# A tile of expert rows shared by two consecutive pairs in the sum into tokens

## The reference

```python
top_val, top_idx = lax.top_k(logits, TOP_K)              # TOP_K = 2, of 8 experts
gates = jax.nn.softmax(top_val, axis=-1)
combine = jnp.sum(jax.nn.one_hot(top_idx, N_EXPERTS) * gates[..., None], axis=1)
for e in range(N_EXPERTS):                               # t is 256 x 1024, experts 3584 wide
    out = out + combine[:, e:e + 1] * (silu(t @ w_gate[e]) * (t @ w_up[e])) @ w_down[e]
```

## Time and profile before

| What | us |
|---|---|
| time, median of 3 runs | 1363.96 |
| lowest and highest of them | 1361.51, 1366.25 |
| time of the profiled execution | 1361.95 |
| its span, first to last instruction | 1360.5 |

### The profile page before, as it was taken

One profiled execution on the slowest core, in us unless ns is written; L12 is line 12 of the kernel. 1 busy time (PEld: TensorE's weight loads), 2 busy tenths in 40 slices (PEclk: granted clock), 3 DMA queues, 4 the chain that ended last, 5 costly groups with the idle time before them and its releaser, 6 DMA issues.

```text
span 1360.5 us, 20505 instructions
## 1 busy us (share of the span) xinstructions
PE 1297.9 (95%) x8957; PEld 811.9 (60%) x8957; DVE 553.3 (41%) x804; ACT 442.7 (33%) x658; POOL 10.8 (1%) x35
## 2 busy tenths in 40 slices
PE   7989999998988999899799999999999999999997
PEld 6777788877777666667666484733333354333343
DVE  5674455545585654646566474410000001200003
ACT  6554444436552553535346263300000000000001
POOL 3000000000000000000000000000000000000000
PEclk9989999999988999899899999999999999999999
DMA  9335555374102999999999999999999999999992
GB/s 333 118 124 185 186 187 186 121 247 145 41 1 89 409 409 390 408 361 395 407 385 407 383 408 402 402 409 409 408 409 396 381 363 347 391 379 404 406 398 82
DMA packets 129067, 418.75 MB, mean 308 GB/s; under 512 B 4248, under 2 KB 8384, under 8 KB 128976
## 3 DMA queue, kind: packets, MB, share of 16 engines
q1 hardware_dynamic: 127872, 416.30, 79.2%
q0 software_dynamic: 544, 1.12, 0.3%
q10 hardware_dynamic: 560, 0.01, 0.0%
HBM read 416.37 MB, written 1.05 MB: 307 GB/s over the span
## 4 chain that ended last, share of the span: by engine, by line
PE 87%; DVE 5%; DMA 3%; ACT 3%; issue 1%; ACTq 0%; SPq 0%; DVEq 0%
PE bank L2036 26%; PE bank L2107 14%; PE bank L1694 13%; PE bank L1695 13%; PE bank L1696 13%; DMA ring<-in_moe_w_down 3%; PE bank L1972 2%; PE bank L1966 2%; PE bank L2055 1%; ACT raw_d L776 1%; DVE lo L1083 1%; DVE mx L1172 1%; DVE raw_d L1169 1%; DVE w_lo L1513 1%; PE bank L1803 1%; PE bank L1744 1%
## 5 line engine op out<-in xcount | busy, mean ns | idle before, releaser
L1513 DVE TENSOR_TENSOR w_lo<-ring,w_hi 128x1024 fp32r<-128x1024 f32 x168 | 202.1, 1224 | 69.5 <-ACT w_hi L711 61.7
L2036 PE MATMUL bank<-ring,late_acts 128*32 128x256 f32 (+3 forms) x1936 | 215.8, 434 | 0.0
L711 ACT ACTIVATE w_hi<-ring 128x1024 fp32r<-128x1024 f32 x168 | 174.9, 1058 | 101.1 <-PE bank L1696 77.8
L1694 PE MATMUL bank<-hi,act_hi 128*128 128x512 f32 (+1 forms) x400 | 156.1, 390 | 12.6 <-DVE lo L1083 6.6
L2036 PEld LDWEIGHTS bank<-ring,late_acts 128*32 128x32 f32 (+1 forms) x1936 | 85.7, 120 | 121.6 <-issue 100.8
L2107 PE MATMUL bank<-ring,at_buf 128*32 128x256 f32 (+1 forms) x1408 | 157.1, 450 | 0.5 <-ACT at_buf L711 0.5
L1695 PE MATMUL bank<-lo,act_hi 128*128 128x512 f32 (+1 forms) x400 | 153.9, 385 | 0.0
L1696 PE MATMUL bank<-hi,act_lo 128*128 128x512 f32 (+1 forms) x400 | 153.8, 384 | 0.0
L711 ACT ACTIVATE at_buf<-bank 128x256 f32<-128x256 f32 (+2 forms) x40 | 18.0, 450 | 412.7 <-PE bank L2055 412.7
L1083 DVE TENSOR_TENSOR lo<-raw_gu,hi 128x1024 fp32r<-128x1024 f32 x96 | 112.4, 1221 | 25.7 <-ACT hi L711 25.0
L1535 DVE TENSOR_TENSOR silu_buf<-silu_buf,bank 128x512 f32<-128x512 f32 (+2 forms) x56 | 29.4, 536 | 225.5 <-PE bank L2036 192.2
(11 more groups left out here) (240 smaller groups left out, 1272.0 us busy)
## 6 DMA issues: line engine op xcount, KB each, us to landing
ring<-in_moe_w_up SPq DMA_DIRECT2D x50, 2048.0 KB, 15.5
ring<-in_moe_w_down SPq DMA_DIRECT2D x49, 2048.0 KB, 15.6
ring<-in_moe_w_gate SPq DMA_DIRECT2D x48, 2048.0 KB, 15.1
raw_gu<-in_w_in SPq DMA_DIRECT2D x7, 2048.0 KB, 13.1
ring_after<-in_moe_w_gate SPq DMA_DIRECT2D x7, 2048.0 KB, 15.8
ring_after<-in_moe_w_down SPq DMA_DIRECT2D x7, 2048.0 KB, 16.9
ring_after<-in_moe_w_up SPq DMA_DIRECT2D x6, 2048.0 KB, 16.8
raw_gu<-in_dense_w_gate SPq DMA_DIRECT2D x5, 2048.0 KB, 8.1
```

Of the source, the lines that this page charges most:

```text
L711: return nc.scalar.activation(out, in_, ACT.Copy, **kw)
L1513: v.tensor_tensor(w_lo[:, n % WP, :], flat(u)[:, q * 1024:(q + 1) * 1024], w_hi[:, n % WP, :], ALU.subtract).then_inc(w_lo_done, 1)
L1694: mm(out, ah, wh, start=start, stop=False, **kw)
L2036: ins = mm(bank[b][c * g.n:(c + 1) * g.n, 0:width], acts[STEPS[s][0]][:, k, g.col:g.col + g.n], by_rows(u, n)[:, kl, c * width:(c + 1) * w ...
```

## The change

Of the slots of two consecutive pairs (0 with 1, and 2 with 3), the second tile is now one and the same. The table `ROW_OF` gives each group (pair, expert, group) its tile and first row. Pair 0 puts its 32 slots of rank 7 and the last 32 of rank 0 in rows 0 to 63 of tile 1, as before. Pair 1 now puts its rank 6 in rows 64 to 127 of it, where it used rows 0 to 63. In pair 2 the 32 odd slots of rank 4 go to rows 96 to 127 of tile 0, and its other 64 stay in tile 1; pair 3 puts its rank 5 in rows 64 to 127 of tile 1.

```diff
+ROW_OF = {(0, 0, 0): (0, 0), (0, 0, 1): (0, 64), (0, 0, 2): (1, 32), (0, 1, 0): (1, 0),
+          (1, 0, 0): (0, 0), (1, 0, 1): (0, 64), (1, 1, 0): (1, 64),
+          (2, 0, 0): (0, 0), (2, 0, 1): (0, 64), (2, 1, 1): (0, 96), (2, 1, 0): (1, 0),
+          (3, 0, 0): (0, 0), (3, 0, 1): (0, 64), (3, 1, 0): (1, 64)}
...
-        self.tile, self.row = w, 64 * i
-        if w == 0 and i == 2:
-            self.tile, self.row = 1, CAPS[PAIRS[p][1]]
+        self.tile, self.row = ROW_OF[p, w, i]
...
     if n < 8:
+        if p % 2 == 1:
+            return ("rows", 0, n - 4) if n >= 4 else None
         return ("rows", n // 4, n % 4) if p > 0 else None
-    if n in (8, 9):
+    if n == 8 or (n == 9 and p % 2 == 1):
         return ("gates", n - 8, 0)
...
-                        if a == 1 and p < NP - 1:
+                        if a == p % 2 and p < NP - 1:
                             build_gsel(p + 1)
...
-                        pe.wait_ge(y_out, 2 * (p - 1) + a + 1)
+                        pe.wait_ge(y_out, 2 * p if p % 2 == 1 or a == 1 else 2 * p - 1)
```

## The result

| Kernel | median of 5 runs, us | lowest, highest |
|---|---|---|
| before | 1364.47 | 1361.51, 1366.25 |
| changed | 1353.88 | 1352.08, 1357.11 |

The ratio is 0.9926 (95% interval 0.9906 to 0.9947), which is 10.1 us less, between 7.2 and 12.8. The forecast was 1356.2, in a range of 1353.8 to 1361.1; the median lies 0.1 us inside its lower end. The profiled execution of the changed kernel took 1353.63 us, 1351.7 of it span.

What follows compares the result with a forecast made beforehand. PE was taken to bound the kernel, with the loads close behind. Terms 3.8 + 4.2 + 0.3 = 8.3 us, less 0.5 for loads, gave 7.8 us less: 1354.1 profiled, 1356.2 against the median, range 1353.8 to 1361.1.

Steps and rivals of the forecast that it cites:

- Row products of pair 1: Four row products (extras 0 to 3) leave PE's stream in pair 1, nothing taking their place: 3.83 us less.
- extra 0: First of pair 1's four removed row products, in step 8 between gate and up products: 0.86 us on the chain.
- More rows contracted: Remaining products contract over 128 rows instead of 64 or 96, in pair 2 and at the end: 0 cost.
- Row products of pair 3: Four row products leave PE's stream in pair 3, at 1.05 us each: 4.2 us less, called safe from the loads.
- Gate turn of pair 2: One turn of gates (two transposes) goes in pair 2, where PE never idles: 0.3 us less.
- That of pair 0: One turn of gates goes in pair 0, ahead of a wait for loads: 0, and 0.3 us at most.
- Turn at the end of step 8: PE's turn of gated values has less work ahead, some 0.4 us cover left: 0 cost, 0.5 us if not.
- Builds moved: In pair 0 DVE's six builds move ahead of two subtractions, with 1.4 us of cover: 0, at most 0.1 us.
- Loads: Pair 1, ahead of its last wide down products: loads nearly follow the faster PE, 0.5 us lost, between 0 and 3.8.
- Rival (a): Loads don't close up; PE waits 3.8 us in pair 1, perhaps at half clock: 1359.5 to 1361.1 us, chance 0.18.
- Rival (b): Loads bound all of the experts' part, so a faster PE only waits more: 1364.0 us, chance 0.07.
- Rival (c): Slower: PE waits at pair 1's wide down products, each wait halving the clock and costing 1.6 us more; chance 0.03.

Runs made afterwards that it cites:

- k128: Kernel before, products summing pairs 0 and 1 padded with zero rows to contract over 128, none removed: 0.81 us less at extras 4 to 7, 0.33 in pair 2.
- before2: The kernel before, unchanged, profiled a second time: 1362.51 us in one run.
- again2: The changed kernel, unchanged, in a third profile: 1353.20 us in its one run.
- again: The changed kernel, unchanged, timed and profiled once more: 1355.26 us, median of 6, against 1362.66 for the kernel before, ratio 0.9942.
- norows1: The changed kernel without the four row products of pair 1 (pair 0's tile 0 not added to the tokens): 1353.68 us in one run.
- late_norows: The changed kernel with DVE's down-sum copies behind step 8's first low pieces and pair 1's four row products left out: 1346.84 us in one run.
- late_before: The kernel before, with DVE's down-sum copies moved behind the low pieces of step 8's first unit: 1357.59 us, ratio 0.9963 to before.

## Why the prediction was right

The sum was 7.8 us off the profiled time, and 8.3 were measured between the two profiled executions (1361.95 to 1353.63), and 10.1 and 7.9 by the ratios of all runs. The mechanism is the one that was named: products leave a PE that hardly stops, and the loads keep up. But the number is better than the terms: on PE 8.8 us were won where 8.3 were forecast, in these two executions none of the 0.5 for the loads was lost, and 0.5 came back outside the span. Step by step:

- **Row products of pair 1, 3.83 forecast.** The intervals gave 0.01 for extra 0 and 2.97 for extras 1 to 3. The three were right (0.86 + 1.05 + 1.06 = 2.97). Extra 0 failed: the chain gave it 0.86 us, but the product covered ACT's silu, and a wait of 0.78 us took its place. The step that failed is the sentence that nothing takes their place, with "followed by wide products, which start without the pause" as the reading of a short entry. The short entry was the sign of the cover.
- **More rows contracted, 0 forecast.** It was a gain of 0.82 us in pair 1 and 0.33 in pair 2, and the eight products at the end took 0.19 less (no run pads those alone). The mistake was to price a product by the duration of its records where its cost lies in the distances to its neighbours.
- These two errors nearly cancel, by luck: -0.86 and +1.34.
- **Row products of pair 3, 4.2 forecast.** 4.23.
- **Gate turn of pair 2, 0.3 forecast.** 0.67 less the 0.33 that k128 shows for the rows: 0.34. **That of pair 0, 0 forecast:** 208.18 and 207.71 for 0 to 39 against 207.80; nothing that can be told.
- **Turn at the end of step 8, 0 forecast.** No wait in PE's timeline of the changed kernel:

```profile
701.06 1.93 PE L2113 MATMUL bank<-ring,at_buf 128*32 128x256 f32 x32
...
702.93 0.66 PE L2061 MATMUL bank<-ident,silu_buf 128*128 128x128 f32 x4
```

- **Builds moved, 0 forecast.** The copy and the subtraction are 3.30 us apart (539.81 to 543.11), as before (537.47 to 540.77 in the earlier trace rows), and DVE still waits 1.54 us in between:

```profile
539.81 0.43 DVE L1485 COPY gselT<-bank 128x256 f32<-128x256 f32 x1 [3.37 <-PE bank L1994]
540.15 1.42 DVE L1466 TENSOR_SCALAR gsel<-iota,slot_r,gate_r 128x64 f32<-128x64 f32 x6
543.11 0.69 DVE L1527 TENSOR_TENSOR at_wide_lo<-bank,at_wide_hi 128x512 fp32r<-128x512 f32 x1 [1.54 <-ACT at_wide_hi L717]
```

- **Loads, 0.5 lost forecast, between 0 and 3.8.** 0 in two profiles and 1.55 in one. The reading of the earlier trace rows was right: the gap between the loads that landed at 755.2 and 762.1 closed (756.3 and 761.5 in the changed kernel). The reading of the earlier trace rows, that no cover at all is left, was true of that one execution only. In before2 there were 2.7 us of it, and the loads needed to follow by less than the 3.8 us: they came 2.0 us earlier in again2, and cover paid the rest. So nothing is lost where the parts of the load lie close, and "again" shows an execution in which the last two were late.

Rival (a), that the loads don't close up, didn't come. The wait in "again", at the place that it named, cost 1.5 us and no clock; its cause was the spread of one load's parts and not a full queue. Rival (b), that the loads bound everything, is excluded by 4.23 us won in pair 3. In pair 1 it is nearly true of the changed kernel, which had 1.3 us left (norows1), and wholly true once DVE's copies are later: late_norows shows products worth 4.3 us leaving for nothing. Rival (c) didn't come: no stretch of PE's work behind 681 us was at half clock in the changed kernel.

The sum has nothing of the start and of the part behind PE. The first row of the table varies by 2.3 us without a pattern. The last is near 7.8 in all kernels with a shared tile and 8.9 to 9.3 in those without; all of that 1.1 us lies behind the last instruction of DVE, and about 0.5 comes back outside the span. Why it goes with the sharing stays open, and it wasn't tried.

## What to carry to other kernels

Before an operation is counted as gained, look at what its successor waits for: if the chain shows it shorter than its neighbours of the same kind, it is probably covering a wait, and moving work into that place is worth more than taking it out of it. Price an operation on a pipelined engine by the distance from the product ahead to the one behind, with and without it, and not by the duration of its record. Where loads run near their limit, measure the cover at the tightest point, from the landing to PE's arrival: it (1.3 us here) says how much more work is worth removing before the loads have to be relieved first. Take it from more than one profile, for the last part of one load can land 2.7 us late in one profile and not in the next.

## What the runs showed of the hardware

- Products over 64 rows between products over 128 rows cost up to 0.28 us more at their borders than the same product over 128 rows, though the records have one duration. Beside products that are themselves over 64 rows (as at 965 us in pair 2) the row product takes 1.05 to 1.06 us to its neighbour in both forms.
- One core drew 409 to 410 GB/s from its loads for tens of microseconds.
- The 16 parts in which a 2 MB load lands lay 2.0 us apart in one profile of a kernel and 4.7 in another (changed and "again", unit 82; 4.3 and 2.2 in the kernel before and before2). What waits for the load waits for the last of them.
- The same short wait can leave the clock alone or halve it. In the kernel before PE waited 1.33 us at 735 and stayed at 1.00. In late_before it waited as long at 730, and behind it the clock stood at 0.50 (1.2 GHz) for 3.4 us, which cost 1.6. PE's timeline and the stretch behind it (columns as in the earlier trace rows) in late_before:

```profile
730.21 0.50 PE L1701 MATMUL bank<-w_hi,wide_hi 128*128 128x512 f32 x1 [1.33 <-DVE w_lo L1513]
...
730.70:733.90 3.20, 3.20 (x10) 2.45 (x9) 2.86 (x3) 1.04 (x1) 0.00 (x0) 0.50 1.03 410
```

  Nor is a longer wait sure to: behind the 2.77 us at 661 us the clock fell in the profile of the kernel before and stayed at 1.00 in that of the changed one (10.69 against 12.03 us in interval 39 to 40). The 3.22 us of late_norows halved it:

```profile
768.89 0.47 PE L1709 MATMUL bank<-w_hi,at_wide_hi 128*128 128x512 f32 x1 [3.22 <-DVE w_lo L1521]
...
768.80:772.80 4.00, 3.91 (x11) 3.08 (x12) 4.00 (x5) 2.58 (x3) 0.00 (x0) 0.58 1.03 410
```

  So a wait's length alone doesn't tell whether the clock falls, and what one profile shows behind a wait is one draw. Of the 2.3 us between the spans of the changed kernel and "again", 1.4 are this (39 to 40) and 1.55 the late load; the other intervals ahead of unit 41 take 0.6 off.
